# A decoder trunk on one core: inner sums over twelve pairs, joins behind the first weight sum, seven products in a second down projection

## The reference

```python
def swiglu(h, w_gate, w_up, w_down):
    return (jax.nn.silu(h @ w_gate) * (h @ w_up)) @ w_down
...
for layer in range(DEPTH):
    h = h + 0.5 * swiglu(rmsnorm(h, ffn1_norm[layer]), ...)
    h = h + mixer(rmsnorm(h, mix_norm[layer]))   # even: GLA and S5, odd: sparse attention
    h = h + cross_attn(rmsnorm(h, xa_norm[layer]), mem_n, ...)
    h = h + 0.5 * swiglu(rmsnorm(h, ffn2_norm[layer]), ...)
return rmsnorm(h, final_norm)
```

## Time and profile before

| | |
|---|---|
| median of three executions | 2114.55 us (2113.4 to 2116.29) |
| the profiled execution | 2116.28 us |
| its span, first to last instruction | 2114.4 us |
| PE, PEld busy | 2100.5 us, 1860.4 us |
| DVE, ACT, POOL busy | 1368.7, 848.8, 1563.7 us |
| granted PE clock | 0.998 of full speed |

### The profile page before, as it was taken

How to read it: one execution, slowest core, us unless ns; L and a number is a source line. 1 busy time by engine, 2 the same in 40 slices (tenths; PEclk the granted TensorE clock), 3 DMA queues, 4 the chain that set the end, 5 groups by cost and what they waited for, 6 DMA issues and landing times. The chain is left out here.

```text
span 2114.4 us, 36869 instructions
## 1 busy us (share of the span) xinstructions
PE 2100.5 (99%) x13238; PEld 1860.4 (88%) x13238; DVE 1368.7 (65%) x2028; ACT 848.8 (40%) x1615; POOL 1563.7 (74%) x1380
## 2 busy tenths in 40 slices
PE   9999999999999999999999999999999999999998
PEld 7899988888888899998889998886878888999987
DVE  6876796695455576664377666456872746789743
ACT  5255312034233355541245552134362434555522
POOL 7778897667974778887778888785757656888874
PEclk9999999999999999999999999999999999999999
DMA  5333333223331233333223333232322222333332
GB/s 200 114 120 111 100 99 121 90 77 100 125 105 53 96 107 108 104 105 120 95 99 102 115 105 101 94 105 71 107 87 92 79 66 93 106 101 102 111 102 80
DMA packets 115422, 215.11 MB, mean 102 GB/s; under 512 B 12832, under 2 KB 14400, under 8 KB 115008
## 3 DMA queue, kind: packets, MB, share of 16 engines
q1 hardware_dynamic: 111024, 202.03, 29.3%
q10 hardware_dynamic: 4240, 10.99, 1.5%
HBM read 208.77 MB, written 4.19 MB: 101 GB/s over the span
## 5 line engine op out<-in xcount | busy, mean ns | idle before, releaser
L600 POOL TENSOR_TENSOR w_split<-w_raw,w_split 128x512 fp32r<-128x512 f32 (+1 forms) x470 | 650.7, 1385 | 40.0 <-ACT w_split L1937 1.1
L688 PE MATMUL ps<-x,w_split 128*128 128x512 f32 (+1 forms) x1702 | 656.0, 385 | 0.7 <-DVE x L2234 0.4
L690 PE MATMUL ps<-x,w_split 128*128 128x512 f32 (+1 forms) x1702 | 649.1, 381 | 0.0
L689 PE MATMUL ps<-x,w_split 128*128 128x512 f32 (+1 forms) x1702 | 648.9, 381 | 0.0
L590 POOL TENSOR_SCALAR w_split<-w_raw 128x512 fp32r<-128x512 f32 x466 | 328.7, 705 | 333.4 <-PE ps L690 316.4
L902 PE MATMUL ps<-x,w_split 128*128 128x264 f32 (+1 forms) x1952 | 549.4, 281 | 3.7 <-DVE ps L2456 3.5
L904 PE MATMUL ps<-x,w_split 128*128 128x264 f32 (+1 forms) x1952 | 548.4, 281 | 0.0
L903 PE MATMUL ps<-x,w_split 128*128 128x264 f32 (+1 forms) x1952 | 547.0, 280 | 0.0
L688 PEld LDWEIGHTS ps<-x,w_split 128*128 128x128 f32 x1702 | 319.8, 188 | 72.3 <-issue 9.4
L633 POOL TENSOR_TENSOR w_split<-w_raw,w_split 128x512 fp32r<-128x512 f32 x216 | 298.6, 1383 | 108.8 <-ACT w_split L1722 108.8
L689 PEld LDWEIGHTS ps<-x,w_split 128*128 128x128 f32 x1702 | 320.0, 188 | 62.2 <-issue 1.4
(11 more groups left out here) (376 smaller groups left out, 2717.1 us busy)
## 6 DMA issues: line engine op xcount, KB each, us to landing
w_raw<-in_stream SPq DMA_DIRECT2D x758, 256.0 KB, 2.7
arena<-in_memT ACTq DMA_DIRECT2D x2, 1024.0 KB, 5.8
s_tables<-kv ACTq DMA_DIRECT2D x4, 512.0 KB, 3.0
arena<-s_tables ACTq DMA_DIRECT2D x4, 512.0 KB, 4.3
out<-h ACTq DMA_DIRECT2D x6, 256.0 KB, 2.7
h<-in_xT SPq DMA_DIRECT2D x4, 256.0 KB, 5.0
h<-in_xT SPq DMA_DIRECT2D x2, 512.0 KB, 6.4
w_raw<-in_stream SPq DMA_DIRECT2D x5, 128.0 KB, 5.1
```

The costliest lines, as they stand in the source:

```text
L600: pool.tensor_tensor(lo, x, hi.bitcast(F32), ALU.subtract).then_inc(split_ready if half else S("half_split"), 1)
L688: pe.matmul(dst, wh, xh, start=start, stop=False)
L689: pe.matmul(dst, wh, xl, start=False, stop=False)
L690: return pe.matmul(dst, wl, xh, start=False, stop=stop)
```

## The change

- `EXTRA` = {1: 4, 3: 4}: f = 1 also takes its first 8 hidden blocks through four more seven-product pairs, and its plain down projection starts at block 8 and has 14 blocks. The buffers of the inner sums are those that held the positions and tables, so the positions are loaded behind the pairs of f = 1 and the tables come behind blocks 12 and 15.
- The eight inner sums are added in pairs 9, 11, 13, 15, 16, 17, 18, 19 and their lower halves made in pairs 10, 12, 14, 16, 17, 18, 19, 20. Both kinds meet in pairs 16 to 19 alone (before: 12 to 18). The first part of a sum waits for six hidden blocks instead of eight.
- In f = 1 and 3, pairs 9 to 23 have both joins ahead of T2's sum.

```diff
-TABLES_BEHIND, SQUARES_BEHIND = (8, 13), 17
-EXTRA = {3: 4}
+TABLES_BEHIND, SQUARES_BEHIND = (12, 15), 17
+EXTRA = {1: 4, 3: 4}
...
-HID_FROM = 11
+HID_LEAD = 10
+HID_ADD = [9, 11, 13, 15, 16, 17, 18, 19]
+HID_LOW = [10, 12, 14, 16, 17, 18, 19, 20]
+JOINS_FIRST = range(HID_ADD[0], FC + 2)
...
                 if f == 1:
-                    for d in range(4, 20):
+                    act.wait_ge(S("m_done"), 3 * SEVEN_BEFORE[f + 1])
+                    act.dma_start(area(A_POS + T).bitcast(I32), pos.to_broadcast([P, T])).then_inc(S("pos_in"), 16)
+                    for d in range(d0 + 4, 20):
...
-                    dve.wait_ge(S("hid_done"), FC * f + 8)
+                    dve.wait_ge(S("hid_done"), FC * f + 6 + 2 * u)
...
-                    if p == HID_FROM:
+                    if p in HID_LOW:
+                        hid_sum_low(HID_LOW.index(p))
+                    if p in HID_ADD:
+                        hid_add(HID_ADD.index(p))
+                    if p == HID_LEAD + 1:
                         hid_lead_low()
-                    if HID_FROM < p <= HID_FROM + 8:
-                        hid_sum_low(p - HID_FROM - 1)
-                    if HID_FROM <= p < HID_FROM + 8:
-                        hid_add(p - HID_FROM)
...
-                    if f in EXTRA and p in (FC - 1, FC):
-                        if p < FC:
+                    if f in EXTRA and p in JOINS_FIRST:
+                        if p == FC - 1:
                             hid_low("A11")
```

More of the change, by code:

```diff
@@ L179 @@
 HID_SUMS = [f"{name}{u}" for u in "ab" for name in ("S1", "S2", "S4", "S3")]
-HID_PARTS = ["lead"] + HID_SUMS + ["A11", "Aa", "Ab"]
-HID_FROM = 11
+HID_PARTS = HID_SUMS[0:1] + ["lead"] + HID_SUMS[1:] + ["A11", "Aa", "Ab"]
+HID_LEAD = 10
+HID_ADD = [9, 11, 13, 15, 16, 17, 18, 19]
+HID_LOW = [10, 12, 14, 16, 17, 18, 19, 20]
+JOINS_FIRST = range(HID_ADD[0], FC + 2)
 SUMS_AT = {1: "S2", 2: "S4", 3: "S3"}
@@ L1791, in seven @@
                         high(p + 1, "B11")
-                    if f in EXTRA and p == HID_FROM - 1:
+                    if f in EXTRA and p == HID_LEAD:
                         hid_lead()
@@ L1797, in seven @@
                     keep(p, "c2")
-                    if f in EXTRA and HID_FROM <= p < HID_FROM + 8:
-                        hid_sum_high(p - HID_FROM)
+                    if f in EXTRA and p in HID_ADD:
+                        hid_sum_high(HID_ADD.index(p))
                     if f in EXTRA and p == FC - 1:
@@ L2191, in _ @@
             norm(3)
-            act.dma_start(area(A_POS + T).bitcast(I32), pos.to_broadcast([P, T])).then_inc(S("pos_in"), 16)
             ffn(1)
```

## The result

The changed kernel takes 2121.01 us (median of 8 executions, 2119.99 to 2122.12), the kernel before 2114.85 beside it (8 executions, 2113.40 to 2117.19): a ratio of 1.0027 with an interval of 1.0018 to 1.0036. It is 6.2 us slower. Forecast were 5.3 us more on the span and a time of 2120.0.

What follows compares the result with a forecast made beforehand. Taken as bound by the matrix engine, busy 2100.5 us (99%). New waits of 6.9 us per feed-forward, less 4.7 (fourth) and 3.8 (second), give +5.3 on 2114.55: 2119.9, said as 2120.0; eight-in-ten range 2108.0 to 2124.0.

Steps and rivals of the forecast that it cites:

- The chain from C22 to T2: Second and fourth feed-forward, pairs 9 to 21: C22 waiting for T3 delays next pair's T2 0.37 us, 4.8 per feed-forward.
- the row of 10.42: Kernel before, pairs with both kinds of inner work: C11 joins 10.42 us apart; their 0.49 loss bounds the 0.37 above.
- The 6.6 us of waits: Kernel before, fourth feed-forward: 23 pairs take 235.0 us against 228.4 when nothing is late, so 6.6 are waits.
- Part 2: Sums spread over twelve pairs, both feed-forwards: taken alone, gains 1.5 us in the fourth and costs 2.0 in the second.
- The term of 1.2 in pair 21: Pair 21, each feed-forward: T1's sum comes 7.82 us behind C22, making C22 late; 1.2 us, bounds 0 and 1.7.
- the forecast's second rival: T1's sum is short where it counts, so neither 1.2 nor 0.94 us arises: about 2115.7 us, chance 0.25.
- The term of 0.94 in pair 24: Pair 24, each feed-forward: leaving the new join order makes C22 late, costing 0.94 us, bounds 0 and 1.4.
- The saved columns, 3.8: Second feed-forward: eight plain down projection blocks, 43.5 us, become four pairs, 39.7 us; saves 3.8 us.
- Tables and positions at nothing: Second feed-forward: later loading of positions and tables costs 0 us, since splits are made three blocks (16.3 us) ahead.
- The sum: Net change over both feed-forwards: +2.2 us in the fourth and +3.1 in the second, together +5.3 us.

Runs made afterwards that it cites:

- The run without sums: Kernel before, with both joins ahead of T2's sum in pairs 6 to 19 of the third feed-forward, which has no inner sums: 2119.60 us, ratio 1.0028.

## Why the prediction was right, step by step

- **The chain from C22 to T2: right**, in mechanism, place and size. 10.30 us was forecast for pairs 10 to 22 and is what seven of them take in the fourth feed-forward. The run without sums shows the order's own price, 0.37; the run with c1 moved shows the way it takes; the run with C12 alone shows which join it is. Pairs 10 to 22 sum to 6.2 us in the fourth feed-forward where 4.8 was forecast. Of the difference 0.8 is pair 12, and 0.5 is that pairs 11 and 17 to 20 cost 0.47 to 0.49: there the vector engine's round is full, and the row of 10.42, taken as the upper bound, was the value. (The 6.6 us of waits that the prediction reads in the kernel before are 0.5 too many, since its window of 235.0 us is wider than the 23 pairs, 234.48; the sum does not use them.)
- **Pair 11 was left out.** Part 2 of the forecast counted pairs with both kinds of inner work and gave the leading halves no term. In pair 11 they take 1.30 us each where they took 0.22, and that comes to 0.8 in the changed kernel and 1.1 in the run with the old joins. Their place behind a sum is not the whole reason, since ahead of it they took 0.86 and 1.32. So Part 2 by itself gave the fourth feed-forward 0.4 and not 1.5 (0.7 without pair 3, whose wait differs between executions).
- **The term of 1.2 in pair 21: wrong.** The start of T1's sum was right (7.93 against 7.82 behind C22). Its length was taken from the nearest rows, 1.67 and 2.13, and it was 0.70, as A11's split was 1.25 and not 2.35: both began in a pause of GpSimd's. That was the forecast's second rival, and it held for this term alone.
- **The term of 0.94 in pair 24: right**, 0.86 and 0.87. Its T1 sums were shorter than the 1.67 taken from the row (1.24 and 1.34), and C22 still came 7.82 us behind C11, as in pair 23 before. Leaving the new order cost the same 0.86 in the run in the third feed-forward.
- **The saved columns, 3.8: right.** Eight blocks went (43.5 us), four pairs of 9.93 came.
- **Tables and positions at nothing: right**, by the same 43.5 us, which the blocks alone account for.
- **The sum**: +2.2 and +3.1 were forecast, +2.5 and +3.7 measured. Two misses, pair 12 (with the full rounds) and pair 21, nearly cancel. That is luck: the total is better than its parts. What stays open is 0.35 in pair 16 of the second feed-forward, where T4's sum in the round before stood 0.52 us instead of 0.17 (the profile names the scalar engine's upper halves, but T2's came as soon behind its sum as in the pair before, 0.72), and some 0.25 in pair 3 of each, a wait that differs between executions of the same code (0.50 to 0.92 in the profiles of this study, once none).

## What to carry to other kernels

A hole in an in-order queue is filled for free only by an instruction that is ready when the hole opens. Look up what the moved instruction waits for and when that ends: C12 was nearly ready (0.36 of waiting), and with it alone in front the two stretches of pairs take 3.8 us less than with neither (464.3 against 468.1); C22 was not, and held work that had been done early before. And follow what stands last behind it to the next engine's queue, where a small copy behind a late one can be the one that the busiest engine waits for.
Extra work that overfills a round costs nothing as long as the lateness doesn't add up beyond the slack of the wait behind it: with C12 alone in front, two such rounds in a row were free, the third and fourth paid 0.45 to 0.49 each, and four of them apart paid nothing.

## What was not expected of the hardware

A vector instruction's length depends on when it starts. The same 128x64 instruction took 0.22 and 1.30 us, T1's sum 0.70 and 1.80, A11's split 1.25 and 2.35. For the shortest the price is the rest of GpSimd's current instruction, so that two tiny steps cost as much as two large ones. A length read from one place can't be carried to another without GpSimd's timeline beside it.
